# Three of four recurrent heads: inverse roots on VectorE by Newton steps, rows scaled on ScalarE

## The reference, cut to what matters

```python
    den = jnp.sum(s, axis=-1) + inter_w * jnp.einsum('bhcid,bhcd->bhci', qc, n_prev)
    h = num / jnp.maximum(jnp.abs(den), jnp.exp(-m_comb))[..., None]
...
    h_ml = rmsnorm(h_ml, ml_head_norm.reshape(ML_HEADS, ML_V))
    h_ml = h_ml * jax.nn.sigmoid(o_ml.astype(jnp.float32)).reshape(B, S, ML_HEADS, ML_V)
```

## Time and profile before

| what | value |
|---|---|
| median of the runs | 1511.37 us |
| the profiled execution: its own time | 1513.8 us |
| its span in the profile | 1512.0 us |
| TensorE matmul busy | 1491.3 us, 99% |
| VectorE, ScalarE, GpSimd busy | 75%, 50%, 41% |
| mean granted TensorE clock | 0.998 |

### The profile page before, as it was taken

One profiled execution on the slowest core, in us unless ns is written; L12 is line 12 of the kernel. 1 busy time (PEld: TensorE's weight loads), 2 busy tenths in 40 slices (PEclk: granted clock), 3 DMA queues, 4 the chain that ended last, 5 costly groups with the idle time before them and its releaser, 6 DMA issues.

```text
span 1512.0 us, 20174 instructions
## 1 busy us (share of the span) xinstructions
PE 1491.3 (99%) x6978; PEld 1231.2 (81%) x6978; DVE 1128.0 (75%) x1872; ACT 751.4 (50%) x1255; POOL 626.8 (41%) x280
## 2 busy tenths in 40 slices
PE   9999999999999999999999999999999999999998
PEld 7888888878888887888888888787778888888887
DVE  5689999997865445776776768788755887777776
ACT  6554333455562345754544345464963745444434
POOL 3455444332334432144444445451534344444451
PEclk9999999999999999999999999999999999999999
DMA  5343233345443323333333123233643432333551
GB/s 212 98 124 99 95 94 95 92 157 157 157 157 98 98 83 112 104 93 97 112 98 109 52 85 97 84 98 93 186 140 105 142 117 90 109 122 114 142 136 56
DMA packets 77026, 170.40 MB, mean 113 GB/s; under 512 B 22660, under 2 KB 39172, under 8 KB 76680
## 3 DMA queue, kind: packets, MB, share of 16 engines
q1 hardware_dynamic: 75920, 165.64, 35.2%
q10 hardware_dynamic: 1016, 3.61, 0.7%
HBM read 154.54 MB, written 14.69 MB: 112 GB/s over the span
## 4 chain that ended last, share of the span: by engine, by line
PE 87%; ACT 4%; DVE 4%; issue 3%; POOL 1%; DMA 1%; SPq 0%; DVEq 0%; ACTq 0%; POOLq 0%
PE bank L795 86%; DMA w_raw<-in_stream 1%; POOL w_lo L655 1%; ACT w_hi L1604 1%; DVE x_sq L2359 0%; ACT l_probs L2129 0%; DVE bias L2441 0%; ACT l_probs L2135 0%; ACT dn_first L1898 0%; POOL res L764 0%; DMA dn_raw<-in_stream 0%; PE bank L1214 0%; DVE res_tok L3421 0%; PE bank L905 0%; ACT ml_square L2080 0%
## 5 line engine op out<-in xcount | busy, mean ns | idle before, releaser
L655 POOL TENSOR_TENSOR w_lo<-w_raw,w_hi 128x1024 fp32r<-128x1024 f32 x191 | 473.2, 2487 | 518.1 <-ACT w_hi L1604 510.4
L795 PE MATMUL bank<-a_hi,w_hi 128*128 128x512 f32 (+1 forms) x1120 | 444.8, 397 | 2.2 <-DVE a_lo L3284 1.8
L795 PE MATMUL bank<-a_hi,w_lo 128*128 128x512 f32 (+1 forms) x1120 | 431.4, 385 | 0.0
L795 PE MATMUL bank<-a_lo,w_hi 128*128 128x512 f32 (+1 forms) x1120 | 431.2, 385 | 0.0
L1604 ACT CAST w_hi<-w_raw 128x1024 fp32r<-128x1024 f32 x199 | 204.6, 1046 | 174.9 <-DMA w_raw<-in_stream 174.5
L795 PEld LDWEIGHTS bank<-a_hi,w_hi 128*128 128x128 f32 x1120 | 210.5, 188 | 49.0 <-issue 4.2
L795 PEld LDWEIGHTS bank<-a_lo,w_hi 128*128 128x128 f32 x1120 | 210.6, 188 | 45.2 <-issue 3.4
L795 PEld LDWEIGHTS bank<-a_hi,w_lo 128*128 128x128 f32 x1120 | 210.4, 188 | 42.6
L667 POOL TENSOR_TENSOR dn_rest<-dn_raw,dn_second 128x1024 fp32r<-128x1024 f32 x39 | 93.7, 2431 | 248.3 <-DVE dn_rest L2734 248.3
L795 PE MATMUL bank<-dn_rest,f_hi 128*128 128x512 f32 x364 | 141.7, 389 | 0.0
L1898 ACT CAST dn_first<-dn_raw 128x1024 fp32r<-128x1024 f32 x54 | 55.6, 1047 | 157.9 <-DVE dn_raw L2715 157.9
(11 more groups left out here) (428 smaller groups left out, 2763.5 us busy)
## 6 DMA issues: line engine op xcount, KB each, us to landing
w_raw<-in_stream SPq DMA_DIRECT2D x199, 512.0 KB, 3.5
dn_raw<-in_stream SPq DMA_DIRECT2D x56, 512.0 KB, 3.6
p_parts<-d_parts SPq DMA_DIRECT2D x8, 640.0 KB, 3.9
d_turned<-p_parts SPq DMA_DIRECT2D x32, 160.0 KB, 3.3
l_turned<-p_parts SPq DMA_DIRECT2D x32, 160.0 KB, 3.1
p_parts<-l_parts SPq DMA_DIRECT2D x8, 384.0 KB, 3.3
res<-in_xT ACTq DMA_DIRECT2D x1, 2048.0 KB, 9.1
p_parts<-l_parts SPq DMA_DIRECT2D x8, 256.0 KB, 2.4
```

The source lines that it names most:

```text
L655: nc.gpsimd.tensor_tensor(w_lo[:, j, :], w_raw[:, j, :], w_hi[:, j, :].bitcast(F32), ALU.subtract).then_inc(w_lo_done, 1)
L795: return nc.tensor.matmul(o, l, r, start=start, stop=stop)
```

## The change

For heads 0, 1 and 2 the square root and the reciprocal become ten instructions on VectorE at step 8: a first estimate out of the bits of the number and three Newton steps of three instructions, each of them waiting for the one before by a semaphore (`chained`). They stand in VectorE's unit in front of the next head's diagonals. For all four heads ScalarE scales the rows at step 9 in place of VectorE; ScalarE's heads are walked in reverse order, so that the scaling stands behind the next head's first decays. The last head keeps `Sqrt` and the reciprocal.

```diff
@@ -220,6 +220,8 @@
+ROOT_SEED = float(0x5F3759DF)
+ROOT_STEPS = 3
@@ -2076,11 +2078,18 @@
                 if st == 7:
                     act.wait_ge(sems["ml_out"], 4 * (h + 1))
+                    if h >= 1:
+                        act.wait_ge(sems["ml_inv"], h)
                     for qb in range(TB):
                         m = A.activation(ml_square[:, qb * P:(qb + 1) * P], ml_block(qb, ML_V), ACT.Square,
                                          accum_out=mcol[:, 2, qb:qb + 1])
                     m.then_inc(sems["ml_sq"], 1)
-                if st == 8:
+                if st == 9:
+                    act.wait_ge(sems["ml_inv"], h + 1)
+                    for qb in range(TB):
+                        m = A.activation(ml_rows[:, qb, :], ml_block(qb, ML_V), ACT.Copy, scale=mcol[:, 3, qb:qb + 1])
+                    m.then_inc(sems["ml_scaled"], 1)
+                if st == 8 and h == ML_HEADS - 1:
                     act.wait_ge(sems["ml_var"], h + 1)
                     A.activation(mcol[:, 3, :], mcol[:, 2, :], ACT.Sqrt).then_inc(sems["ml_root"], 1)
@@ -2099,7 +2108,7 @@
                 if n in cast_at and n < LATE_CASTS:
                     round_to(cast_at[n])
-                for h in range(ML_HEADS):
+                for h in reversed(range(ML_HEADS)):
                     ml_step(h, n - ML_START - ML_EVERY * h)
@@ -3110,6 +3119,19 @@
+            def inverse_root(h):
+                part, x, y = mcol[:, 0, :], mcol[:, 2, :], mcol[:, 3, :]
+                dve.wait_ge(sems["ml_var"], h + 1)
+                chained(V.tensor_scalar(y.bitcast(I32), x.bitcast(I32), -0.5, ROOT_SEED, ALU.mult, ALU.add))
+                for i in range(ROOT_STEPS):
+                    chained(V.scalar_tensor_tensor(out=part, in0=y, scalar=-0.5, in1=y, op0=ALU.mult, op1=ALU.mult))
+                    chained(V.tensor_tensor(part, part, x, ALU.mult))
+                    m = V.scalar_tensor_tensor(out=y, in0=part, scalar=1.5, in1=y, op0=ALU.add, op1=ALU.mult)
+                    if i < ROOT_STEPS - 1:
+                        chained(m)
+                    else:
+                        m.then_inc(sems["ml_inv"], 1)
+
             def ml_step(h, st):
@@ -3119,13 +3141,12 @@
+                if st == 8 and h < ML_HEADS - 1:
+                    inverse_root(h)
                 if st == 9:
-                    dve.wait_ge(sems["ml_root"], h + 1)
-                    V.reciprocal(mcol[:, 3, :], mcol[:, 3, :]).then_inc(sems["ml_inv"], 1)
-                    dve.wait_ge(sems["ml_inv"], h + 1)
-                    for qb in range(TB):
-                        m = V.tensor_scalar(ml_rows[:, qb, :], ml_block(qb, ML_V), mcol[:, 3, qb:qb + 1], None, ALU.mult)
-                    m.then_inc(sems["ml_scaled"], 1)
+                    if h == ML_HEADS - 1:
+                        dve.wait_ge(sems["ml_root"], 1)
+                        V.reciprocal(mcol[:, 3, :], mcol[:, 3, :]).then_inc(sems["ml_inv"], 1)
```

## The result

The changed kernel took 1515.18 us (median of 10 runs, 1513.77 to 1516.94) against 1511.76 us before (10 runs, 1510.81 to 1514.22), ratio 1.0020 with a 95% interval of [1.0010, 1.0029]: slower by about 3 us, 1.5 to 4.4 (the two medians lie 3.4 us apart, the two means 3.1). The forecast was 1514.9.

The account below looks back on a forecast made before the run. TensorE's matmuls, busy 99% of the span, were taken as the bound, its waits set by late ScalarE. Terms 2.1 + 1.6 - 0.2 = +3.5 us on the 1511.4 us median gave 1514.9 us, range 1510.8 to 1516.8.

Parts of the forecast that it names:

- The ten steps: Root on VectorE: ten dependent instructions starting 0.20 us apart take 1.96 us, bounds 0.8 and 4.7 us.
- Head 0: Units 11 to 14: root in front of the diagonals delays scaling, decays and rows; turn, gate and values +0.5 us.
- Head 1: Units 17 to 21: lateness carried on, TensorE idle 2.9 us before the turn; +2.1 us in all, 0.5 included.
- The clock: Behind unit 21: the 2.9 us hole drops TensorE's clock to 1.2 GHz, costing 1.6 us, bounds 0 and 1.6.
- Head 2: Units 25 to 28: table load gone, gate and values some 0.2 us early, -0.2 us; holes and clock fall stay.
- the rival with the clock up: No fall behind unit 21; GpSimd's additions hold VectorE's columns, head 2 +0.9 us; 1513.3 to 1514.4 us; chance 0.38.
- Head 3 and the added wait: Last head's rows on idle ScalarE, and the squares' wait for a root seven units old: both cost nothing.
- GpSimd's later release: GpSimd let go later behind each set of diagonals, in head 1 by 3.4 us: nothing on TensorE.
- The bounds: Forecast's own limits, from clock price 0 to 1.6 us and rows 0.9 to 1.6 us twice: 1513.3 to 1516.3 us.
- The rival with cheap steps: Root's steps start 0.08 us apart, root takes 0.8 us: together -3.3 us, 1508.1; chance 0.12.
- the one with loads that stay: On ScalarE, Copy or Square needs its own table, two loads per head remain: +6 us or more; chance 0.02.
- The block that reaches further: On top of the clock's fall, GpSimd's hold on VectorE reaches further: 1516 to 1518 us; chance 0.06.

Follow-up runs that it names:

- the two further ones: The changed kernel unaltered, profiled in two more executions: 1514.78 and 1515.11 us, one run each.
- e5: Changed kernel with GpSimd's 8 additions of units 23 to 26 moved last, behind the low part of head 3: 1514.19 us, 1.0017 of before.
- e3: Changed kernel with the root moved one unit, to step 9, behind diagonals and inverse of the row sums: 1522.73 us, 1.0062 of before.
- e2: Kernel before with only the rows scaled on ScalarE behind the decays, Sqrt and reciprocal kept: 1515.15 us, 1.0016 of before.

## Why the prediction was right and where it was wrong

The time, the direction and the chain through heads 0 and 1 came as forecast; of the sum of 3.5 us two terms were wrong and stood against each other. That the median came within 0.3 us of the forecast is in part luck. Times below have the 0.27 us of the start taken off.

- **The ten steps**: 1.96 us forecast, 1.91 measured, 0.20 us apart. Right.
- **The rows on ScalarE**: 1.1 us forecast, 1.12 measured.
- **Head 0**: scaling of unit 12 at 1065.85, measured 1065.78, ScalarE idle 3.15 us; +0.5 us forecast, 0.49 measured.
- **Head 1**: squares 1.5 us late, measured 1.55; scaling of unit 19 at 1087.65, measured 1087.65; score at 1091.2, measured 1091.19; +2.1 us, measured 2.09; hole 2.9, measured 2.84.
- **The clock**: the step that failed. It said that a fall of 1.6 us comes behind unit 21 and that the one behind unit 28 stays. The profiled execution had no fall behind unit 21; the two further ones had it there and lost the other. A fall more than in the profiled execution of before was seen in this stage in none of the three. The reasoning from the length of the holes (2.9 is more than 1.25 and 0.78) is what the runs refute. Over all runs some 0.9 us of falls may still be in the loss (the estimate above), since before has its fall only in some; the term of 1.6 us took it as always there.
- **Head 2**: -0.2 us forecast, +0.65 measured. This is the rival with the clock up: it had VectorE's columns stand until GpSimd's last addition ends, put at 1105.75 us, measured 1105.78; its head 2 was +0.9 us. The sizes were off both ways: with the additions out of the way (e5) the values of unit 28 start 1.40 us later than before, seen from the stage's start, of which head 1 gives 2.09. So head 2 gives -0.7 there and not -0.2, and the block costs 1.3 us and not 1.1. Of the ten steps, nine of which the prediction said could be caught, none was (0.13 to 0.16 us): the one column instruction in front of them took the whole hold.
- **Head 3 and the added wait**: nothing, as forecast. **GpSimd's later release** (3.4 us in head 1, as forecast) was not nothing: nobody waited for its low parts, but it is what put the additions beside head 2's columns.
- **The bounds**: the upper one of the forecast itself, 1516.3 us, counts the rows' 0.9 to 1.6 us as 0.7 too much, twice; against the 1.1 in the sum it is 0.5, and the bound 1515.9. The lower one leaves the rows out; with them it is 1512.9.

So the profiled execution went the way of the rival with 0.38, 2.1 + 0.65 us; its stage is 2.70 us longer. The executions with the fall at unit 21 have a stage only 1.5 and 1.6 us longer than the profiled one of before, which had a fall too. How much of the 3 us over the runs (interval 1.5 to 4.4) hangs on how often each kernel meets a fall is known only by the estimate above. The rival with cheap steps and the one with loads that stay are out: the steps stand 0.20 us apart, and the loads left are one for `Sqrt` and its return. The block that reaches further, on top of the fall, was not seen either: in the two executions with the fall behind unit 21 the columns were held 0.38 and 0.35 us.

Of the two pages cited: the drain that the Trainium skill, page "ScalarE: Activation LUTs", section "What ACT_TABLE_LOAD costs", adds to each load is not in the trace, where the `Sqrt` starts 0.01 us behind its load; heads 0 and 1, worked out with 1.28 us a load, came within 0.1 us. The lock of the page "SBUF — State Buffer" (the Trainium skill, section "SBUF: two separate sides") agrees with the long instructions of two SBUF inputs above, to 0.02 us at their ends. The held `tensor_scalar` of e3 has one SBUF input, and that part of the rule, as cited, does not cover it.

## What to carry to other kernels

An engine's load is no measure of what a removed operation gives: ask what the instruction that replaces it stands in front of. Here ten short steps in front of one reciprocal of 0.16 us turned 2.7 us of table loads and `Sqrt` into 3.15 us of idle time on the same engine. A chain of small dependent instructions did best here on the engine that was waiting anyway, and the place of each of VectorE's instructions with two SBUF operands is to be checked against what GpSimd does at that time.

## What the runs showed of the hardware that was not expected

- TensorE's clock with the same program and a hole in unit 21 equal to 0.03 us fell behind unit 21 in two executions and behind unit 28 in one; with a hole of 2.98 us (e2) it did not fall in the profiled one.
- A VectorE instruction of 4 columns waited 1.88 us for GpSimd, longer than one of its additions (1.25 us): it did not get in between two that stood in line. The first step of the root, `tensor_scalar` on int32 with one SBUF operand, was held as well (1.66 us in e3).
- Dependent instructions of 128x4 cost 0.20 us each on VectorE and 0.28 us on GpSimd, start to start: only 0.08 us apart.
